# Two small edits in a macaron transformer kernel: the mixing step three units later, and each quarter of x loaded by one request

## The chip, the cores and the metric

The kernel runs on one core of one Trainium2 chip, as one launch. Five engines work side by side and meet at semaphores: TensorE (PE; its weight loads are listed as PEld), VectorE (DVE), ScalarE (ACT), GpSimd (POOL) and SyncE (SP), which here only issues DMA requests. The metric is device time in microseconds, the median of some runs; lower is better. The profile is of one execution, and its times start with the program's span.

## The reference, cut to what matters

Two layers act on x of shape 256 x 1024. Each is a half-weighted SwiGLU feed-forward, a mixer, and a second feed-forward; a norm ends the whole. All weights are f32 in HBM.

```python
for l in range(2):
    x = x + 0.5 * swiglu(rms_norm(x, g1[l]), w_up1[l], w_down1[l])     # 1024 -> 2 x 2816 -> 1024
    x = x + hybrid_mixer(rms_norm(x, g2[l]), ...)                      # proj = h @ w_in, 1024 -> 5888
    x = x + 0.5 * swiglu(rms_norm(x, g3[l]), w_up2[l], w_down2[l])
return rms_norm(x, final_norm)

# in hybrid_mixer: 12 dilated heads in 3 groups of 4, each with its log-sum-exp, and 8 neighbourhood heads
mix_w = softmax(stack(lses), axis=0)                  # weights of the 3 groups, one per head and row
ya = sum(mix_w[..., None] * stack(outs), axis=0)      # dilated branch, 256 columns
yb = neighbourhood_attention(qb, kb, vb, rel_bias)    # 512 columns
merged = sigmoid(gate_a) * (ya @ w_a) + sigmoid(gate_b) * (yb @ w_b)
return merged @ w_out
```

## The kernel before

**Units.** All weights stream through three slots of 128 x 2048 f32 (1 MB a unit). SyncE requests a unit in two DMAs into `raw` (L394), ScalarE rounds it to `w_hi` (L629), VectorE takes the remainder `w_lo = raw - w_hi` (L864), and TensorE multiplies three times (hi x hi, hi x lo, lo x hi: L1207 to L1209 in the mixer, L1270 to L1273 in the feed-forwards). A slot is given back by `split_free` when TensorE has used it. A feed-forward has 33 units, a mixer 30, numbered m = 0 to 29 in each layer.

**The mixer.** Units 0 to 22 are the projection. Attention is put between them: the tables `SCORES_AT`, `TURN_AT`, `TURN_MID`, `VALUES_AT` and `VALUES_MID` say in which unit the scores of a pair of heads, the transposes of their probabilities and the products with v stand, on every engine. Each engine executes its own list in order. Between them VectorE masks scores (L1047), copies the turned probabilities to SBUF (`probs_turned`, L1020; TensorE's products L1442 and its next transposes L1421 wait for that copy), and reads products (`products_read`, L1058 for dilated and L1067 for neighbourhood pairs).

**The mixing.** In unit `MIX_AT`, `mix_weights` (L1082 to L1091, eight small instructions on VectorE, with one Exp on ScalarE, L794, in the middle) makes the group weights `mix_d`. GpSimd waits for them and makes the dilated branch's y in three instructions over all heads (L597, L600, L603). TensorE needs that y in unit `Y_AT` = 22, where it transposes y (L1489). GpSimd has nothing else to do in that time.

**The start.** x lies in SBUF with its rows regrouped by residue modulo 4: partition j of run r holds row 4 j + r, and a run has 64 rows. A quarter of x is 128 partitions (two runs) by 512 columns, 256 KB, and `load_x` (L376) requests it in two DMAs, one a run:

```python
eng.dma_start(runs[i * RUN:(i + 1) * RUN, :], residues(x_in)[r, :, n * NB:(n + 1) * NB])   # 64 x 512 to 64 x 512
```

SyncE requests quarter 0, then the first half of weight block 0 (`first_part(0, 0)`, L463, 512 KB in two requests), quarter 2, `first_part(1, 0)`, quarter 3, `first_part(0, 1)`, `first_part(1, 1)`, then unit 2. Quarter 1 is requested by ScalarE, on its own queue. TensorE transposes the quarters (L1245) in the order 0, 1, 2, with five idle-filling products (`spin`, L1238) after 1 and after 2, and then makes the first products of block 0; quarter 3 is transposed after these, and then the products of block 1's first half. For the second halves it needs `first_part(0, 1)` rounded (`first_hi`, L817) and quarter 3 in `a_both` (L637, L889).

**Requests on GpSimd's queue that a later section looks at.** `na_mask` (L553) and `bias_rows` (L582) are read through a source whose outermost dimension is 4; `v_near` (L592) through one whose outermost dimension is 16:

```python
src = bass.AP(consts.tensor, ..., [[STRIDE * C_ALL, NA_COLS // STRIDE], [0, NA_HEADS], [1, NA_KCOLS]])   # na_mask: 4 x 8 x 32
src = bass.AP(bias_kinds.tensor, ..., [[row * P // STRIDE, STRIDE], [row, P // STRIDE], [1, NA_KEYS]])   # bias_rows: 4 x 32 x 128
near = v_rows[l].rearrange("(g s) n -> g s n", s=RUN // ROWS_N)[:, s0:s0 + NA_KCOLS // STRIDE, :]        # v_near: 16 x 8 x 512
```

Of the kernel before, what the change touches and what calls it, by code (L numbers as in the profile page):

```python
# [12 lines left out]
P = 128  # L13
# [21 lines left out]
RUN = SEQ // STRIDE  # L35
# [7 lines left out]
NB = 512  # L43
# [60 lines left out]
TURN_MID = {12: 3, 14: 5, 17: 7, 19: 9}  # L104
VALUES_AT = {12: (1,), 13: (2, 3), 16: (4, 5), 18: (6, 7), 20: (8, 9)}
VALUES_MID = {10: (0,)}
MIX_AT = 16


def first_of(p):  # L110
# [9 lines left out]
def build(nc, x_in, gains, w_up, w_down, w_in, rel_bias, w_a, w_b, w_out, consts, out):  # L120
# [5 lines left out]
    with ExitStack() as ctx:  # L126
        def sb(name, shape, dt=F32):
            return ctx.enter_context(nc.sbuf_tensor(name, shape, dt))

        def sem(name):  # L130
            return ctx.enter_context(nc.semaphore(name))
# [7 lines left out]
        x = sb("x", [P, TT, D])  # L139
# [77 lines left out]
        x_loaded = [sem(f"x_loaded{g}") for g in range(4)]  # L217
# [91 lines left out]
        def residues(rows):  # L309

            return rows.rearrange("(j r) d -> r j d", r=STRIDE)
# [58 lines left out]
        def load_x(eng, g):  # L370

            t, n = GROUP4[g]
            runs = x[:, t, n * NB:(n + 1) * NB]
            for i in range(P // RUN):
                r = t * (P // RUN) + i
                eng.dma_start(runs[i * RUN:(i + 1) * RUN, :], residues(x_in)[r, :, n * NB:(n + 1) * NB]).then_inc(x_loaded[g], 16)  # L376

        def x_ready(eng, ph, g):

            if ph == 0:  # L380
                eng.wait_ge(x_loaded[g], 16 * P // RUN)
            else:
                eng.wait_ge(x_updated, (ph - 1) * 4 + g + 1)

# [4 lines left out]
        def _(sp):  # L389
# [67 lines left out]
            def first_part(a, h):  # L457

                src = w_up[0].rearrange("l (k p) n -> l p k n", p=P)
                to = raw[a][:, :].rearrange("p (k n) -> p k n", n=FC)  # L460
                for k in (4 * h, 4 * h + 2):
                    arrived = first_arrived if (a, k) == (0, 0) else part_arrived[2 * a + h]
                    sp.dma_start(to[:, k:k + 2, :], src[0, :, k:k + 2, a * D_FF:a * D_FF + FC]).then_inc(arrived, 16)  # L463

            def feed_forward(f, l, at):
# [8 lines left out]
                unit(n0 + F_UNITS - 1, 2, down_unit(f, l, CHUNKS - 1))  # L474

            load_x(sp, 0)
            first_part(0, 0)
            load_x(sp, 2)
            first_part(1, 0)
            load_x(sp, 3)  # L480
            first_part(0, 1)
            first_part(1, 1)
# [31 lines left out]
            for t in range(TT):  # L514
                sp.wait_ge(result_ready, t + 1)
                r = t * P // RUN
# [96 lines left out]
        def _(act):  # L613
            act.dma_start(ident, consts[:, C_IDENT:C_ALL]).then_inc(ident_loaded, 16)
            act.dma_start(gain_rows[0:DEPTH * PHASES * KT, :],
                          gains[0:LAST, :].rearrange("g (k p) -> (g k) p", p=P)).then_inc(gain_rows_loaded, 16)
            load_x(act, 1)

            def hi(l, at, u, c=None):

# [20 lines left out]
            def sum_squares(ph, g):  # L641

                t, n = groups(ph)[g]
                x_ready(act, ph, g)
                if g >= 2:
                    act.wait_ge(squares_done, ph * 4 + g - 1)
                act.activation(squares[:, g % 2 * NB:(g % 2 + 1) * NB], x[:, t, n * NB:(n + 1) * NB], ACT.Square,
                               scale=(1 if ph == LAST else 2) * D ** -0.5,
                               accum_out=half_sums[:, n, t:t + 1]).then_inc(squares_done, 1)
# [77 lines left out]
            def mixer(l):  # L727
                ph = l * PHASES + 1
                input_begin(l, ph, M_AT)
                for m in range(M_UNITS):  # L730
# [42 lines left out]
                    for j, i in enumerate(QK_CHUNKS):  # L773
                        if m == chunk_steps(i)[-1] + 2:
                            act.wait_ge(qkT_done, l * 5 + j + 1)
                            for s in range(2):
# [14 lines left out]
                                act.activation(dst, ft, ACT.Copy, scale=HD ** -0.5 if is_q else 1.0).then_inc(qkT_read, 1)  # L791
                    if m == MIX_AT:
                        act.wait_ge(mix_exp_in, l + 1)
# [49 lines left out]
            for t in range(TT):  # L843
                act.wait_ge(result_ready, t + 1)
                r = t * P // RUN + 1
# [5 lines left out]
        def _(dve):  # L851
# [200 lines left out]
            def products_read(l, p):  # L1052

                at = product_at(2 * p, 0)
                src = bank[OB][:, at:at + 2 * TT * HD].rearrange("p (h t d) -> p h t d", h=2, t=TT)
                if p < DIL_PAIRS:
                    dve.wait_ge(pv_done, l * HEADS + 2 * end_of(p))
                    dve.tensor_copy(o_dil[:, 2 * p:2 * p + 2, :, :], src).then_inc(o_read, 1)  # L1058
                    return
                j = p - DIL_PAIRS  # L1060
                dve.wait_ge(o_read, l * PAIRS + p)
                dve.reciprocal(rden[:, :, :], den[:, 2 * p:2 * p + 2, :]).then_inc(rden_done, 1)
                dve.wait_ge(rden_done, l * (PAIRS - DIL_PAIRS) + j + 1)
                dve.wait_ge(pv_done, l * HEADS + 2 * end_of(p))
                at = GROUP_HEADS * HD + 2 * j * HD
                dst = y[:, :, at:at + 2 * HD].rearrange("p t (h d) -> p h t d", h=2)
                dve.tensor_tensor(dst, src, rden[:, :, :].unsqueeze(3).to_broadcast([P, 2, TT, HD]),  # L1067
                                  ALU.mult).then_inc(o_read, 1)

            def mix_weights(l):  # L1070


                n = [0]
                tops = top[:, 0:DIL_HEADS, :].rearrange("p (g h) t -> p g (h t)", g=GROUPS)
                dens = den[:, 0:DIL_HEADS, :].rearrange("p (g h) t -> p g (h t)", g=GROUPS)

                def chained(ins):
                    ins.then_inc(mix_chain, 1)
                    n[0] += 1
                    dve.wait_ge(mix_chain, l * 6 + n[0])  # L1080
                peak = mix[:, 1, :]
                chained(dve.tensor_tensor(mix[:, 0, :], tops[:, 0, :], tops[:, 1, :], ALU.max))  # L1082
                chained(dve.tensor_tensor(peak, mix[:, 0, :], tops[:, 2, :], ALU.max))
                dve.tensor_tensor(mix_d[:, :, :], tops, peak.unsqueeze(1).to_broadcast([P, GROUPS, GROUP_HEADS * TT]),
                                  ALU.subtract).then_inc(mix_exp_in, 1)
                dve.wait_ge(mix_exp, l + 1)
                chained(dve.tensor_tensor(mix_d[:, :, :], mix_e[:, :, :], dens, ALU.mult))
                chained(dve.tensor_tensor(mix[:, 2, :], mix_d[:, 0, :], mix_d[:, 1, :], ALU.add))
                chained(dve.tensor_tensor(mix[:, 3, :], mix[:, 2, :], mix_d[:, 2, :], ALU.add))
                chained(dve.reciprocal(mix[:, 4, :], mix[:, 3, :]))  # L1090
                dve.tensor_tensor(mix_d[:, :, :], mix_e[:, :, :],  # L1091
                                  mix[:, 4, :].unsqueeze(1).to_broadcast([P, GROUPS, GROUP_HEADS * TT]),
                                  ALU.mult).then_inc(mix_ready, 1)
# [19 lines left out]
            def mixer(l):  # L1113
# [3 lines left out]
                for m in range(M_UNITS):  # L1117
# [20 lines left out]
                    for p in VALUES_MID.get(m, ()):  # L1138
                        products_read(l, p)
                    if m == MIX_AT:  # L1140
                        mix_weights(l)
                    if m == Y_AT:
                        for j in range(3):
                            dve.wait_ge(yT_hi_done, l * 3 + j + 1)
                            for (dst, src), (upper, _) in zip(yT_parts(yT_lo, j), yT_parts(yT_hi, j)):
                                half = dve.tensor_tensor(dst, src, upper.bitcast(F32), ALU.subtract)
                            half.then_inc(yT_lo_done, 1)
# [56 lines left out]
        def _(pe):  # L1204
# [35 lines left out]
            def input_transposes(ph, g):  # L1240
                t, n = GROUP4[g]
                x_ready(pe, ph, g)
                for j in range(4):
                    c = n * NB + j * P
                    tr = pe.transpose(bank[TR[g]][:, j * P:(j + 1) * P], x[:, t, c:c + P], ident)  # L1245
                tr.then_inc(xT_done, 1)
# [397 lines left out]
```

## Time and profile before

| | us |
|---|---|
| median of 3 runs | 1149.88 (1149.08 to 1150.02) |
| the profiled execution | 1150.65 |
| its span | 1148.8 |
| PE busy in the span | 1134.7 (99%) |
| DVE busy | 766.4 (67%) |
| ACT busy | 583.8 (51%) |
| POOL busy | 76.6 (7%) |
| mean granted TensorE clock | 0.998 of full speed |
| DMA, all queues | 214.34 MB, mean 187 GB/s |

A busy time is the sum over an engine's instructions. PE is busy nearly all the time, so what it waits for, and how long, is where a change of order can act; the other engines' idle time costs nothing by itself. `spin` products count as busy, though they do no work of the reference.

### The profile page before, as it was taken

What the parts mean: (1) busy time and instruction counts of PE and PEld (TensorE: products, weight loads), DVE (VectorE), ACT (ScalarE), POOL (GpSimd) and SP (SyncE); (2) the same over time, 40 slices, a digit from 0 to 9 for tenths busy, and PEclk for the clock granted to TensorE, in tenths of its full rate; (3) what the DMA queues carried; (4) which work ended last, traced back from release to release, by engine and by line L of the source; (5) the groups of instructions that cost most, each with busy time, mean ns of one, the idle gap of its engine ahead of it and who ended that gap; (6) DMA issues with size and microseconds to landing.
All of it is one profiled execution on the core that took longest, in us unless ns stands there. A gap on an engine that the chain in (4) does not pass through costs nothing.

```text
span 1148.8 us, 17172 instructions
## 1 busy us (share of the span) xinstructions
PE 1134.7 (99%) x6707; PEld 955.3 (83%) x6707; DVE 766.4 (67%) x981; ACT 583.8 (51%) x781; POOL 76.6 (7%) x116
## 2 busy tenths in 40 slices
PE   8999999999999999999999999999999999999997
PEld 6888888888878888888888888888887888888886
DVE  5866667756666676666686666677566577666665
ACT  6444445555544654444474444465555545544442
POOL 3622100000110000000000000000003000000000
PEclk9999999999999999999999999999999999999999
DMA  9866654744544565556556555656446546655551
GB/s 288 276 208 229 205 191 147 256 150 145 191 161 145 183 220 183 184 190 207 171 165 216 183 183 185 201 189 199 152 143 198 202 131 201 202 196 184 184 182 37
DMA packets 148246, 214.34 MB, mean 187 GB/s; under 512 B 9344, under 2 KB 114016, under 8 KB 147936
## 3 DMA queue, kind: packets, MB, share of 16 engines
q1 hardware_dynamic: 142960, 205.28, 53.9%
q0 software_dynamic: 4560, 6.97, 2.1%
q10 hardware_dynamic: 672, 1.37, 0.4%
q8 instruction: 34, 0.56, 0.2%
q14 instruction: 20, 0.16, 0.0%
HBM read 210.75 MB, written 5.12 MB: 188 GB/s over the span
## 4 chain that ended last, share of the span: by engine, by line
PE 94%; DVE 2%; issue 1%; ACT 1%; DMA 1%; SPq 0%; POOLq 0%; POOL 0%; DVEq 0%; ACTq 0%
PE banks L1273 25%; PE banks L1207 16%; PE banks L1209 15%; PE banks L1208 15%; PE banks L1271 14%; PE banks L1270 3%; PE banks L1421 1%; PE banks L1384 1%; PE banks L1245 1%; PE banks L1407 1%; PE banks L1453 1%; DMA raw<-ffn_w_up_dram 1%; DVE w_lo L864 1%; ACT w_hi L629 1%; DVE probs L1047 0%
## 5 line engine op out<-in xcount | busy, mean ns | idle before, releaser
L864 DVE TENSOR_TENSOR w_lo<-raw,w_hi 128x2048 fp32r<-128x2048 f32 x190 | 438.8, 2310 | 192.7 <-ACT w_hi L629 192.4
L629 ACT ACTIVATE w_hi<-raw 128x2048 fp32r<-128x2048 f32 x190 | 363.6, 1915 | 212.2 <-PE banks L1209 210.1
L1273 PE MATMUL banks<-a_both,w_hi 128*128 128x512 f32 x1232 | 439.4, 396 | 0.0
L1271 PE MATMUL banks<-a_both,w_lo 128*128 128x256 f32 x1408 | 364.3, 279 | 0.7 <-DVE a_both L889 0.7
L1271 PEld LDWEIGHTS banks<-a_both,w_lo 128*128 128x128 f32 x1408 | 265.4, 189 | 15.7 <-issue 1.0
L1273 PEld LDWEIGHTS banks<-a_both,w_hi 128*128 128x128 f32 x1232 | 231.2, 188 | 47.3
L1207 PE MATMUL banks<-w_hi,a_both 128*128 128x512 f32 (+1 forms) x448 | 176.6, 394 | 0.0
L1209 PE MATMUL banks<-w_hi,a_both 128*128 128x512 f32 (+1 forms) x448 | 171.6, 383 | 0.0
L1208 PE MATMUL banks<-w_lo,a_both 128*128 128x512 f32 (+1 forms) x448 | 171.2, 382 | 0.0
L1207 PE MATMUL banks<-w_hi,hT_hi 128*128 128x512 f32 x320 | 125.0, 390 | 0.0
L1209 PE MATMUL banks<-w_hi,hT_lo 128*128 128x512 f32 x320 | 124.5, 389 | 0.0
L1208 PE MATMUL banks<-w_lo,hT_hi 128*128 128x512 f32 x320 | 124.5, 389 | 0.0
L1209 PEld LDWEIGHTS banks<-w_hi,a_both 128*128 128x128 f32 x448 | 84.2, 188 | 17.0
L1207 PEld LDWEIGHTS banks<-w_hi,a_both 128*128 128x128 f32 x448 | 84.3, 188 | 16.3 <-issue 1.3
L1208 PEld LDWEIGHTS banks<-w_lo,a_both 128*128 128x128 f32 x448 | 84.4, 189 | 14.6
L687 ACT ACTIVATE gates<-banks 128x512 f32<-128x512 f32 x44 | 26.3, 598 | 118.1 <-PE banks L1273 118.1
L694 ACT ACTIVATE gates<-banks 128x512 f32<-128x512 f32 x44 | 26.4, 600 | 101.7 <-PE banks L1273 101.7
L1209 PEld LDWEIGHTS banks<-w_hi,hT_lo 128*128 128x128 f32 x320 | 60.1, 188 | 12.7
L1208 PEld LDWEIGHTS banks<-w_lo,hT_hi 128*128 128x128 f32 x320 | 60.1, 188 | 12.6
L1270 PE MATMUL banks<-a_both,w_hi 128*128 128x512 f32 x176 | 70.1, 398 | 0.0
L1207 PEld LDWEIGHTS banks<-w_hi,hT_hi 128*128 128x128 f32 x320 | 60.1, 188 | 10.8
L937 DVE TENSOR_TENSOR gates<-banks,gates 128x512 f32<-128x512 f32 x44 | 30.4, 691 | 47.5 <-ACT gates L687 47.5
(119 smaller groups left out, 927.4 us busy)
## 6 DMA issues: line engine op xcount, KB each, us to landing
raw<-ffn_w_up_dram SPq DMA_DIRECT2D x172, 512.0 KB, 4.2
raw<-w_in_dram SPq DMA_DIRECT2D x92, 512.0 KB, 4.5
raw<-ffn_w_down_dram SPq DMA_DIRECT2D x88, 512.0 KB, 4.0
raw<-w_out_dram SPq DMA_DIRECT2D x16, 512.0 KB, 4.3
raw<-w_branch_b_dram SPq DMA_DIRECT2D x8, 512.0 KB, 4.4
raw<-ffn_w_up_dram SPq DMA_DIRECT2D x8, 256.0 KB, 5.9
bias_rows<-bias_kinds POOLq DMA_DIRECT2D x32, 64.0 KB, 4.0
bias<-bias_rows SPq DMA_DIRECT2D x2, 1024.0 KB, 7.2
```

The costliest lines, as they stand in the source:

```text
L629: act.activation(w_hi[slot][:, :], raw[slot][:, :], ACT.Copy).then_inc(hi_done, 1)
L687: act.activation(u_low, U_BANKS[:, :, SEQ:2 * SEQ], ACT.Copy).then_inc(u_low_done, 1)
L694: act.activation(v_low, V_BANKS[:, :, SEQ:2 * SEQ], ACT.Copy).then_inc(v_low_done, 1)
L864: dve.tensor_tensor(w_lo[slot][:, :], raw[slot][:, :], w_hi[slot][:, :].bitcast(F32), ALU.subtract).then_inc(lo_done, 1)
L937: dve.tensor_tensor(u_sum, U_BANKS[:, :, 0:SEQ], u_low, ALU.add).then_inc(u_read, 1)
L1207: pe.matmul(dst, s_hi, m_hi, start=start, stop=False)
L1208: pe.matmul(dst, s_hi, m_lo, start=False, stop=False)
L1209: return pe.matmul(dst, s_lo, m_hi, start=False, stop=stop)
L1245: tr = pe.transpose(bank[TR[g]][:, j * P:(j + 1) * P], x[:, t, c:c + P], ident)
L1270: mm = pe.matmul(pair[:, b, :], w, both, start=True, stop=False)
L1271: mm = pe.matmul(pair[:, b, 0:SEQ], w_lo[slot][:, at:at + P], a_hi[:, k, :], start=False, stop=False)
L1273: mm = pe.matmul(pair[:, b, :], w, both, start=False, stop=k == KT - 1)
```

## The change

It has two independent parts. `MIX_AT` goes from 16 to 19, so that the group weights are made at the end of unit 19, and GpSimd's three instructions follow them. And `load_x` makes one request for a quarter in place of two; quarter 1 is requested by SyncE right behind quarter 0, and no longer by ScalarE.

```diff
-MIX_AT = 16
+MIX_AT = 19
@@ load_x
             t, n = GROUP4[g]
-            runs = x[:, t, n * NB:(n + 1) * NB]
-            for i in range(P // RUN):
-                r = t * (P // RUN) + i
-                eng.dma_start(runs[i * RUN:(i + 1) * RUN, :], residues(x_in)[r, :, n * NB:(n + 1) * NB]).then_inc(x_loaded[g], 16)
+            r = t * (P // RUN)
+            rows = residues(x_in)[r:r + P // RUN, :, n * NB:(n + 1) * NB]
+            eng.dma_start(x[:, t, n * NB:(n + 1) * NB], rows).then_inc(x_loaded[g], 16)
@@ x_ready
-                eng.wait_ge(x_loaded[g], 16 * P // RUN)
+                eng.wait_ge(x_loaded[g], 16)
@@ SyncE
             load_x(sp, 0)
+            load_x(sp, 1)
             first_part(0, 0)
@@ ScalarE
-            load_x(act, 1)
```

The source of a request before is 64 rows of 512; the source of one after is 2 x 64 x 512 (run, row, column), and its destination 128 partitions of 512.

On VectorE, around units 16 and 17 of the first mixer, before: `mix`, `mix_d` are the group weights, `probsT` the turned probabilities.

```order
L1058 COPY o_dil<-banks 128x256 x2
L864 TENSOR_TENSOR w_lo<-raw,w_hi 128x2048
L1082 TENSOR_TENSOR mix<-top 128x8
L1083 TENSOR_TENSOR mix<-mix,top 128x8
L1084 TENSOR_TENSOR mix_d<-top,mix 128x24
L1087 TENSOR_TENSOR mix_d<-mix_e,den 128x24
L1088 TENSOR_TENSOR mix<-mix_d 128x8
L1089 TENSOR_TENSOR mix<-mix,mix_d 128x8
L1090 RECIPROCAL mix<-mix 128x8
L1091 TENSOR_TENSOR mix_d<-mix_e,mix 128x24
L1020 COPY probsT<-banks 128x512
L864 TENSOR_TENSOR w_lo<-raw,w_hi 128x2048
```

After, the same place (line numbers are one less):

```order
L1057 COPY o_dil<-banks 128x256 x2
L863 TENSOR_TENSOR w_lo<-raw,w_hi 128x2048
L1019 COPY probsT<-banks 128x512
L863 TENSOR_TENSOR w_lo<-raw,w_hi 128x2048
L1019 COPY probsT<-banks 128x512
```

And after, at the end of unit 19, where the eight instructions now stand:

```order
L1019 COPY probsT<-banks 128x512
L1081 TENSOR_TENSOR mix<-top 128x8
L1082 TENSOR_TENSOR mix<-mix,top 128x8
L1083 TENSOR_TENSOR mix_d<-top,mix 128x24
L1086 TENSOR_TENSOR mix_d<-mix_e,den 128x24
L1087 TENSOR_TENSOR mix<-mix_d 128x8
L1088 TENSOR_TENSOR mix<-mix,mix_d 128x8
L1089 RECIPROCAL mix<-mix 128x8
L1090 TENSOR_TENSOR mix_d<-mix_e,mix 128x24
L1061 RECIPROCAL rden<-den 128x4
L1066 TENSOR_TENSOR y<-banks,rden 128x2x2x64
```

They moved from ahead of the copies and the split of unit 17 to a place behind the last copy of unit 19 and ahead of unit 20's reading of products.

SyncE's first requests, before:

```order
L376 DMA x<-x_dram 64x512 x2
L463 DMA raw<-ffn_w_up_dram 128x2x256 x2
L376 DMA x<-x_dram 64x512 x2
L463 DMA raw<-ffn_w_up_dram 128x2x256 x2
L376 DMA x<-x_dram 64x512 x2
L463 DMA raw<-ffn_w_up_dram 128x2x256 x4
```

And after:

```order
L375 DMA x<-x_dram 128x1x512 x2
L462 DMA raw<-ffn_w_up_dram 128x2x256 x2
L375 DMA x<-x_dram 128x1x512
L462 DMA raw<-ffn_w_up_dram 128x2x256 x2
L375 DMA x<-x_dram 128x1x512
L462 DMA raw<-ffn_w_up_dram 128x2x256 x4
```

The first row is now quarters 0 and 1, one request each (the shape shown is the destination's).

## Rows read from the trace of the kernel before

**Rows 1.** The page: busy us, share of the span, instructions.

```profile
PE 1134.7 (99%) x6707; PEld 955.3 (83%) x6707; DVE 766.4 (67%) x981; ACT 583.8 (51%) x781; POOL 76.6 (7%) x116
```

**Rows 2.** Waits of PE by cause: us in total, times, longest.

```profile
PE banks L1245 <- DMA x<-x_dram: 2.0, 2, 1.6
PE banks L1442 <- DVE probsT L1020: 1.8, 2, 0.9
...
PE banks L1421 <- DVE probsT L1020: 0.5, 2, 0.3
```

**Rows 3.** Timeline of PE, first mixer: start, us, engine, line, operation.

```profile
314.10 0.39 PE L1208 MATMUL banks<-w_lo,a_both 128*128 128x512 f32 x1
314.32 0.39 PE L1209 MATMUL banks<-w_hi,a_both 128*128 128x512 f32 x1
314.98 0.63 PE L1421 MATMUL banks<-cst,probs 128*128 128x128 f32 x4 [0.27 <-DVE probsT L1020]
...
318.30 0.65 PE L1442 MATMUL banks<-v_near,probsT 128*32 128x64 f32 x32
319.87 0.65 PE L1442 MATMUL banks<-v_near,probsT 128*32 128x64 f32 x32 [0.92 <-DVE probsT L1020]
...
333.58 1.10 PE L1442 MATMUL banks<-v_near,probsT 128*32 128x64 f32 x64
...
344.27 0.92 PE L1489 MATMUL banks<-cst,y 128*128 128x128 f32 x7
```

**Rows 4.** Timeline of DVE, first mixer, units 16 to 20.

```profile
310.11 2.28 DVE L864 TENSOR_TENSOR w_lo<-raw,w_hi 128x2048 fp32r<-128x2048 f32 x1
...
314.04 0.18 DVE L1091 TENSOR_TENSOR mix_d<-mix_e,mix 128x24 f32<-128x24 f32 x1
...
314.98 4.23 DVE L864 TENSOR_TENSOR w_lo<-raw,w_hi 128x2048 fp32r<-128x2048 f32 x1
319.14 0.68 DVE L1020 COPY probsT<-banks 128x512 f32<-128x512 f32 x1
...
334.82 0.42 DVE L1067 TENSOR_TENSOR y<-banks,rden 128x256 f32<-128x256 f32 x1 [2.79 <-PE banks L1442]
```

**Rows 5.** Timeline of POOL in the same stretch.

```profile
314.30 2.76 POOL L597 TENSOR_TENSOR o_dil<-o_dil,mix_d 128x1536 f32<-128x1536 f32 x1 [7.53 <-DVE mix_d L1091]
317.14 3.20 POOL L600 TENSOR_TENSOR o_dil<-o_dil 128x512 f32<-128x512 f32 x1
320.42 1.27 POOL L603 TENSOR_TENSOR y<-o_dil 128x512 f32<-128x512 f32 x1
```

**Rows 6.** Stretches of the start: PE, PEld, DVE, ACT, POOL busy, clock, DMA share, GB/s.

```profile
8.00:10.00 2.00, 1.63 (x10) 0.88 (x9) 0.97 (x5) 2.00 (x6) 0.00 (x0) 1.00 1.11 300
12.00:14.00 2.00, 2.00 (x13) 1.71 (x13) 1.23 (x1) 2.00 (x8) 0.00 (x0) 1.00 1.09 383
```

**Rows 7.** DMA queues, 305 to 312 us: packets, MB, share of 16 engines.

```profile
q0 software_dynamic: 320, 1.05, 50.1%
```

**Rows 8.** The same view, 55.5 to 58 us.

```profile
q0 software_dynamic: 316, 0.26, 40.6%
```

**Rows 9.** The same view, 33.4 to 34.2 us, with its packet sizes.

```profile
DMA packets 98, 0.21 MB, mean 262 GB/s; under 512 B 44, under 2 KB 48, under 8 KB 98
...
q0 software_dynamic: 32, 0.00, 7.8%
```

**Rows 10.** x's first request, issued at 0.76: us to landing.

```profile
DMA to landing us min/median/max: 2.9/2.9/2.9
```

**Rows 11.** Timelines of PE and ACT at the start.

```profile
9.41 0.66 PE L1245 MATMUL banks<-cst,x 128*128 128x128 f32 x4 [0.37 <-DMA x<-x_dram]
11.04 0.47 PE L1270 MATMUL banks<-a_both,w_hi 128*128 128x512 f32 x1
...
14.53 1.06 ACT L817 ACTIVATE w_hi<-raw 128x1024 fp32r<-128x1024 f32 x1
...
18.04 0.36 PE L1271 MATMUL banks<-a_both,w_lo 128*128 128x256 f32 x1 [0.70 <-DVE a_both L889]
```

## Prediction

> **What bounds the kernel now.** I read the page's busy line first: PE is busy 1134.7 of 1148.8 us [rows 1], so only what delays PE can move the time, by at most the 14.1 us that are left and whatever a new wait adds. Second, the waits of PE by cause [rows 2]. At the start PE waits for x (2.0 us in two pieces), and in each of the two mixers it waits for VectorE's copies of turned probabilities (L1442, L1421). No row has PE waiting for weights. Once started PE streams, so a delay at the start goes through to the end unshortened, and so does a wait removed from a mixer.
>
> **Part one: the mixing leaves unit 16.** In the timeline of PE [rows 3] the two transposes' neighbours show the price. L1421 starts at 314.98, 0.66 after the product ahead of it, where that one started 0.22 after its own predecessor: 0.43 lost, to the nearest step. The first half of L1442 starts at 318.30 and the second at 319.87, 1.57 later; all 64 of such products take 1.10 at 333.58, so half take 0.55: 1.02 lost. Together 1.45 a mixer, and rows 2 count these waits twice, so 2.9 us.
>
> Why VectorE was late [rows 4]: the eight small instructions hold it from the end of a split at 312.3 to 314.22 (1.9 us), ahead of the copy that L1421 wants. Then the split at 314.98 takes 4.23 where the one at 310.11 takes 2.28. What is beside it: GpSimd's L597 starts at 314.30 the moment the weights are there, runs 2.76, and its L600, a third of the size, takes 3.20, against 1.27 of the equally large L603 that stands beside an idle VectorE [rows 5]. VectorE and GpSimd hold each other up. So the copy that L1442 wants starts only at 319.14. Without mixing in unit 16 the copy runs at 312.3 to 313.0, the split follows and ends by 315.4, and the last copy is done at 316.1, where PE wants it at about 318.4: both waits go, with 2 us to spare. The split's input w_hi comes earlier too, since ScalarE's Exp of the mixing stood ahead of its rounding.
>
> What is late next: nothing in units 17 and 18, since PE's following items have no wait row at all. At the new place, the end of unit 19, VectorE waits 2.79 us for PE (ahead of L1067) [rows 4], and the 1.9 us fit into that; behind it in its queue stand unit 20's reading of products and the split of unit 22, which PE wants a unit and a half later. GpSimd is the one with a date. Everything there is 1.45 earlier: VectorE is free at 334.82 - 2.79 - 1.45 = 330.6, the weights are ready at 332.5, GpSimd needs 7.4 as before (314.30 to 321.69, with both engines' collisions in it), so y is there at 339.9; PE wants it at 344.27 - 1.45 = 342.8 [rows 3]. The margin is 2.9 us. I cost the new place at nothing; if that cover went, it costs what exceeds 2.9, in each mixer. Bounds of part one: -2.9 and, with both collisions moved onto something that PE wants, 0. I take -2.9, since the rows ahead of and behind both places are PE's own.
>
> **Part two: the requests for x.** What it saves on the issuing side is small: three request slots of SyncE and two of ScalarE, about 0.6 us each, in a stretch where the 16 DMA engines are full (share 1.11 and 1.09 in [rows 6]). With the same spreading over the engines I would give it between 0 and -1 us, as the quarters' requests come earlier but their bytes don't move faster.
>
> The point is the spreading. The source of a request was 64 rows; now its outermost dimension is 2 (two runs of 64 rows). The trace has no such request on SyncE's queue, but it has on GpSimd's. Four requests of `v_near`, 16 x 8 rows, 256 KB each, make 320 packets for 1.05 MB [rows 7]. Four of `bias_rows`, 4 x 32 rows, 64 KB each, make 316 (and some on the window's edge) for 0.26 MB [rows 8]: as many packets for a quarter of the bytes. And one of `na_mask`, outermost 4, 4 KB, makes 32 packets [rows 9], while of all packets in that window just 48 - 44 = 4 are between 512 B and 2 KB: the 4 KB are in four pieces, and the rest carry nothing. So the number of engines that carry data is that of the outermost dimension where it is under 16. That is GpSimd's queue, and that SyncE's does the same is my choice; by it each quarter of x goes through 2 of 16 engines.
>
> The Trainium skill says it for both: in "DMA: Bandwidth & Descriptors", "Why a DMA increments its semaphore by 16 and not by 1", the number of engines is the largest up to 16 that divides the slowest dimension over 1 of both access patterns; of 2 and 128 that is 2, on the lowest-numbered engines. The trace agrees for 4 (rows 8, 9), and no run here yet shows it for 2. If its rule held on GpSimd's queue alone, the sum would be the rival's of 1146.5 below.
>
> Price, as work of the two engines, which serve their requests in order. In 12 to 14 us the 16 move 383 GB/s, 23.9 each [rows 6]. A quarter is 131 072 B an engine: 5.48 us. A pair of weight requests spread over 16 gives each 32 768 B: 1.37. The first request of x took 2.9 [rows 10], of which 8192 B at this rate are 0.34, so 2.56 are fixed. Landings: quarter 0 at 0.76 + 2.56 + 5.48 = 8.8; quarter 1 14.3; block 0's first half 15.7; quarter 2 21.1; block 1's 22.5; quarter 3 28.0; `first_part(0, 1)` 29.4; `first_part(1, 1)` 30.7; unit 2 (1 MB, 2.74) 33.5. The rest of each request, on 14 engines, is there long before.
>
> What PE makes of it [rows 11]: its first products come 1.63 behind quarter 2, at 22.8 (before 11.04), and are done before quarter 3 is there. Then the chain that ended last before: ScalarE rounds `first_part(0, 1)`, scales quarter 3, VectorE makes the remainder, PE goes on at 18.04, 3.51 after the 14.53 at which the rounding began. Now 29.4 + 3.5 = 32.9. The delay is 14.8. Unit 2 at 33.5 comes 0.6 behind that point, and PE wants it only after two more half blocks, so it adds nothing, and from there on all requests wait for PE's progress as before. Bounds of the rate an engine reaches: 18.8 GB/s from 8 to 10 us, a stretch with x in it (300/16), gives a quarter 6.99 and a pair 1.74, and a delay of 22.0; from above, a share of 1.09 to 1.11 says that packets overlap within an engine, and one that has no neighbours might gain as much once more, 26.5, which gives a quarter 4.95, a pair 1.24 and a delay of 12.3. I take 23.9, measured where the queues are never short of work and hold no x.
>
> **Sum.** -2.9 + 14.8 = +11.9 against the profiled execution's span, 1148.8 to 1160.7, its time 1150.65 to 1162.5. That execution is 0.8 over the median of the runs, so the median goes from 1149.9 to **1161.8**.
>
> **The rivals.**
> *Sixteen engines all the same* (faster). SyncE's queue would spread 128 rows by the destination, or by rows flattened. For it: all requests of SyncE in the trace keep the engines full, and none shows fillers. Against: [rows 8, 9]. Then PE gets -2.9 and up to -1 at the start: 1146.0 to 1147.0, say 1146.5.
> *TensorE at its lower level.* The granted clock is 1.00 in every stretch of the start, with PE's waits for x up to 1.6 us [rows 2, 6]. Now it idles about 5 us between quarters. Its work from 11.04 to 18.04 is 7.0 less the wait of 0.70 [rows 11], two parts of some 3 us. At 1.2 instead of 2.4 GHz each takes 6: the first ends at 28.8, hidden up to 0.8 behind quarter 3; the second at 35, 2.1 after 32.9; if the next is slow too, 3 more. 1163.9 to 1166.9, say 1165. The Trainium skill's "TensorE: Matmul & The Clock Gate", Part 1, has such a fall for an idle array; that it lasts is not to be read from here.
> *Slow engines*: each of the two at 18.8 GB/s, as in the crowded stretch; +22.0 - 2.9: 1169.
> *y comes late*: GpSimd is held up beyond 10.3 us at its new place by VectorE's splits and reads, and PE waits at unit 22 what it no longer waits at 17 and 18. It decides from the margin of 2.9. With part two's price: up to 1164.7.
>
> **Chances.** Forecast 0.63, its own range 1158 to 1166; lower level 0.11; slow engines 0.06; y late 0.03; sixteen engines 0.15; smaller mixtures 0.02. The range 1155 to 1170 holds all cases but the sixteen engines and tails. A measurement of this kernel can tell 0.2% (2.3 us) from no change: faster 0.14, same 0.02 (a smaller price that cancels part one), slower 0.84.
>
> **What would show it.** Right: the requests of x take 8 us and more to land, PE's first L1270 at 21 to 24 us instead of 11.04, PE's stretch of waits ends at about 33 instead of 18.04; fewer packets of 4 B on SyncE's queue in the first microseconds; waits of L1442 and L1421 for `probsT` gone from the list; the split behind the first copy of unit 17 takes 2.3; GpSimd starts L597 at about 332.5 + 14.8 and the L1489 that follows waits for nothing. Wrong: x landing within 5 us (then the rival of 1146.5), a granted clock under 1.00 in the first 35 us with products 0.46 apart, a new wait of L1489 for `y`, or a PE that waits for `w_lo` behind unit 2.

## The result and the profile after

| | before | after |
|---|---|---|
| median, us | 1149.82 (1149.08 to 1150.02, 4 runs) | 1161.45 (1161.36 to 1162.62, 4 runs) |
| profiled execution: its span | 1148.8 | 1159.6 |
| mean granted TensorE clock | 0.998 | 0.992 |

The ratio is 1.0102 with a 95% interval of 1.0088 to 1.0116: slower by 11.6 us, where 1161.8 was predicted. The rows below are of the profile after; its line numbers are mostly one less than before.

Busy time by engine on the page, against [rows 1]:

```profile
PE 1137.1 (98%) x6707; PEld 956.9 (83%) x6707; DVE 764.7 (66%) x981; ACT 583.4 (50%) x781; POOL 77.8 (7%) x116
```

PE has as many instructions, and the span grew by 10.8 while PE's busy time grew by 2.4: it waits. The waits of PE by cause, against [rows 2]:

```profile
PE banks L1244 <- DMA x<-x_dram: 11.4, 4, 3.9
PE banks L1237 <- DVE warm L852: 1.2, 1, 1.2
PE banks L1270 <- DVE a_both L888: 1.2, 1, 1.2
PE banks L1588 <- DMA gain_rows<-gains_dram: 0.9, 1, 0.9
```

The wait for x went from 2.0 us in two pieces to 11.4 in four, one per quarter. Both rows for `probsT` are gone, and none for `y` has come. PE's timeline at the start, against [rows 11]:

```profile
9.51 1.12 PE L1244 MATMUL banks<-cst,x 128*128 128x128 f32 x4 [3.85 <-DMA x<-x_dram]
14.41 1.11 PE L1244 MATMUL banks<-cst,x 128*128 128x128 f32 x4 [3.79 <-DMA x<-x_dram]
...
20.88 0.92 PE L1244 MATMUL banks<-cst,x 128*128 128x128 f32 x4 [3.22 <-DMA x<-x_dram]
...
23.37 0.99 PE L1269 MATMUL banks<-a_both,w_hi 128*128 128x512 f32 x1
...
27.60 0.66 PE L1244 MATMUL banks<-cst,x 128*128 128x128 f32 x4 [0.53 <-DMA x<-x_dram]
...
32.27 0.36 PE L1270 MATMUL banks<-a_both,w_lo 128*128 128x256 f32 x1 [1.20 <-DVE a_both L888]
```

Quarter after quarter is there 4.9 us or more behind the last. The last row is the end of the waits, at 18.04 before: 14.23 later. What released it is the same chain as before (ScalarE rounds `first_part(0, 1)` and scales quarter 3, VectorE makes the remainders). In ScalarE's timeline:

```profile
28.77 1.06 ACT L816 ACTIVATE w_hi<-raw 128x1024 fp32r<-128x1024 f32 x1 [3.34 <-DMA raw<-ffn_w_up_dram]
```

`first_part(0, 1)` is there at 28.77, and PE goes on 3.50 later (3.51 before). One thing differs: here ScalarE waited for the landing, and before its rounding at 14.53 waited for nothing. The stretches of the start show why, against [rows 6] (the same columns):

```profile
8.00:10.00 2.00, 0.49 (x3) 0.50 (x4) 0.00 (x0) 0.00 (x0) 0.00 (x0) 0.50 0.46 160
10.00:12.00 2.00, 0.62 (x3) 0.22 (x2) 0.02 (x1) 1.14 (x4) 0.00 (x0) 0.50 0.13 51
...
16.00:18.00 2.00, 1.66 (x4) 0.29 (x2) 1.26 (x5) 1.74 (x5) 0.00 (x0) 0.57 0.13 51
18.00:20.00 2.00, 0.00 (x0) 0.00 (x0) 1.06 (x2) 0.00 (x0) 0.00 (x0) 1.00 0.51 146
```

A DMA share of 0.13 is two of 16 engines, moving 51 GB/s together, where the share was 1.1 before. (0.13 is what two engines give if each is busy all the time; that it is two is counted in e5 to e7.) The DMA queues from 10 to 12 us, the view of [rows 7 to 9]:

```profile
DMA packets 50, 0.10 MB, mean 51 GB/s; under 512 B 0, under 2 KB 0, under 8 KB 50
```

Only rows of x of 2 KB move: 25 an engine in 2 us, 25.6 GB/s each. The same rows show what the prediction had as a rival: the granted clock is 0.50, TensorE's lower level of 1.2 GHz, in much of the time between quarters (it reads 1.00 from 18 to 20 us, behind 1.66 us of work).

SyncE's timeline has something nobody asked for:

```profile
0.75 1.30 SPq L375 DMA_DIRECT2D x<-x_dram  x2
2.09 5.07 SPq L462 DMA_DIRECT2D raw<-ffn_w_up_dram  x2
7.20 1.26 SPq L375 DMA_DIRECT2D x<-x_dram  x1
8.51 4.97 SPq L462 DMA_DIRECT2D raw<-ffn_w_up_dram  x2
13.52 1.16 SPq L375 DMA_DIRECT2D x<-x_dram  x1
```

Two weight requests took 1.10 us to issue before (2.02 to 3.12), and take 5.07 now: SyncE stands at a request, it seems while the two engines work off what is queued. Quarter 2 is asked for only at 7.20 and quarter 3 at 13.52. That raised the question of whether the engines or SyncE's stalls cost the time (run e11).

In the first mixer, VectorE's timeline, against [rows 4]:

```profile
326.20 0.68 DVE L1019 COPY probsT<-banks 128x512 f32<-128x512 f32 x1
326.80 2.28 DVE L863 TENSOR_TENSOR w_lo<-raw,w_hi 128x2048 fp32r<-128x2048 f32 x1
...
348.15 2.96 DVE L863 TENSOR_TENSOR w_lo<-raw,w_hi 128x2048 fp32r<-128x2048 f32 x1
```

The split between the copies takes 2.28 and no longer 4.23. GpSimd's three, against [rows 5], and PE's y, against the last of [rows 3]:

```profile
346.20 2.76 POOL L597 TENSOR_TENSOR o_dil<-o_dil,mix_d 128x1536 f32<-128x1536 f32 x1 [25.50 <-DVE mix_d L1090]
349.04 3.23 POOL L600 TENSOR_TENSOR o_dil<-o_dil 128x512 f32<-128x512 f32 x1
352.35 1.30 POOL L603 TENSOR_TENSOR y<-o_dil 128x512 f32<-128x512 f32 x1
```

```profile
356.59 1.47 PE L1488 MATMUL banks<-cst,y 128*128 128x128 f32 x12
```

y is there at 353.65 and wanted at 356.59 without a wait: a margin of 2.94. The collision moved with the mixing, to a split (348.15, 2.96) that nobody waits for.

### The profile page after: what moved, and what is told of

Same layout as the page of the kernel before. It is cut to its first block, busy times and chain, and to the rows that moved or that the text cites. A ratio compares the mean times of both kernels' runs of the same rounds, so it can differ in the third digit from the quotient of the medians.

```text
span 1159.6 us, 17168 instructions
## 1 busy us (share of the span) xinstructions
PE 1137.1 (98%) x6707; PEld 956.9 (83%) x6707; DVE 764.7 (66%) x981; ACT 583.4 (50%) x781; POOL 77.8 (7%) x116
## 2 busy tenths in 40 slices
DMA packets 148126, 214.34 MB, mean 185 GB/s; under 512 B 9224, under 2 KB 113896, under 8 KB 147816
## 4 chain that ended last, share of the span: by engine, by line
PE 96%; SPq 1%; DMA 1%; DVE 0%; issue 0%; ACT 0%; POOLq 0%; POOL 0%; DVEq 0%
PE banks L1272 25%; PE banks L1206 16%; PE banks L1208 16%; PE banks L1207 16%; PE banks L1270 14%; PE banks L1269 3%; SPq L462 1%; PE banks L1420 1%; DMA raw<-ffn_w_up_dram 1%; PE banks L1383 1%; PE banks L1244 1%; PE banks L1406 1%; PE banks L1452 1%; PE banks L1395 0%; PE banks L1441 0%
## 5 line engine op out<-in xcount | busy, mean ns | idle before, releaser
L1206 PEld LDWEIGHTS banks<-w_hi,hT_hi 128*128 128x128 f32 x320 | 60.1, 188 | 10.8
```

Source lines behind the costliest of these rows:

```text
L1206: pe.matmul(dst, s_hi, m_hi, start=start, stop=False)
```

## The experiments

Each median stands beside that of the kernel before from runs on the same chip. PE's restart is the start of the product with which PE went on at 18.04 before, in the profiled execution of each kernel.

| run | median, us | before | ratio (95%) | PE's restart |
|---|---|---|---|---|
| e1_mix19 | 1147.18 | 1150.14 | 0.9974 (0.9965 to 0.9984) | 17.75 |
| e2_xonly | 1165.38 | 1150.14 | 1.0132 (1.0117 to 1.0146) | 33.07 |
| e3_pool_late | 1149.16 | 1150.14 | 0.9993 (0.9984 to 1.0002) | 17.78 |
| e4_mix20 | 1155.35 | 1150.14 | 1.0052 (1.0040 to 1.0064) | 18.10 |
| e5_outer4 | 1154.46 | 1150.16 | 1.0038 (1.0024 to 1.0052) | 23.82 |
| e6_outer8 | 1148.88 | 1150.16 | 0.9991 (0.9981 to 1.0000) | 20.43 |
| e7_outer16 | 1146.34 | 1150.16 | 0.9970 (0.9960 to 0.9981) | 17.31 |
| e8_split2_sp | 1146.95 | 1150.16 | 0.9974 (0.9965 to 0.9984) | 17.52 |
| e9_warm_after | 1161.67 | 1150.23 | 1.0100 (1.0085 to 1.0116) | 33.80 |
| e10_outer8_warm | 1148.90 | 1150.23 | 0.9992 (0.9983 to 1.0001) | 20.60 |
| e11_x_on_act | 1167.53 | 1150.23 | 1.0149 (1.0134 to 1.0165) | 38.56 |
| e12_one_merged | 1152.80 | 1150.23 | 1.0023 (1.0013 to 1.0032) | 23.88 |

### e1_mix19: the mixing alone

```diff
-MIX_AT = 16
+MIX_AT = 19
```

(on the kernel before)

> The kernel before with MIX_AT = 19 alone, the loads of x untouched. Theory (the two parts are independent and TensorE streams between them): both mixers lose the waits of L1442 and L1421 for probsT, so -2.9 to -3.2 us against before, about 1146.7, and the split behind unit 17's first copy takes 2.3 us. Rival (the gain seen after is a side effect of the later start, which gave the weight stream a lead): under 1 us, and waits for probsT remain.

Measured: 2.96 us faster. The waits of PE in full, but for one on the `spin` weights:

```profile
PE banks L1245 <- DMA x<-x_dram: 2.1, 2, 1.3
...
PE banks L1271 <- DVE a_both L889: 0.7, 1, 0.7
```

Nothing of the mixer is left in the list. By start times of the same products, the two transposes win 0.45 and the two products 1.15 in each mixer. Part one is a gain by itself.

### e2_xonly: the requests alone

```diff
-MIX_AT = 19
+MIX_AT = 16
```

(on the kernel after)

> The changed kernel with MIX_AT back at 16, so that only the requests for x differ from before. Theory: +14.2 us against before (TensorE's restart at 32.3 instead of 18.0), about 1164.0, with the two waits for probsT in each mixer as before. Rival (part of the later start is absorbed by slack in the first feed-forward): under +12.

Measured: 15.24 us slower than before; PE restarts 15.03 later. Its list of waits has the mixer's back:

```profile
PE banks L1244 <- DMA x<-x_dram: 11.4, 4, 4.0
PE banks L1441 <- DVE probsT L1019: 1.8, 2, 0.9
...
PE banks L1420 <- DVE probsT L1019: 0.5, 2, 0.3
```

The parts add within 0.7: 15.24 - 2.96 = 12.3 against 11.6 for both. The text had 14.2.

### e3_pool_late: GpSimd out of the way, VectorE's mixing left in place

```diff
-                pool.wait_ge(o_read, l * PAIRS + DIL_PAIRS)
+                pool.wait_ge(o_read, l * PAIRS + PAIRS - 1)
```

(on the kernel before: GpSimd starts on y only when VectorE has read the products of all pairs but one; the eight small instructions stay in unit 16)

> The kernel before (mixing in unit 16, old loads), but GpSimd's three mixing instructions also wait until the ninth pair of products has been read (unit 20). Separates the two parts of VectorE's lateness. Theory (the collision with GpSimd makes L1442 wait, the eight small instructions make L1421 wait): the split at unit 17 takes 2.3 instead of 4.2, the wait of L1442 goes (1.0 a mixer), the wait of L1421 stays (0.3 to 0.4 a mixer): -2.0 us against before. Rival (the eight instructions and ScalarE's Exp alone make the delay): no gain, -0.3 to 0.

Measured: 0.98 us less in the median, with an interval that just includes no change, and 1.5 less in the span of the profiled execution. The text had 2.0. What it shows is in the trace. VectorE's timeline:

```profile
314.68 2.29 DVE L864 TENSOR_TENSOR w_lo<-raw,w_hi 128x2048 fp32r<-128x2048 f32 x1 [0.15 <-ACT w_hi L629]
...
334.38 4.47 DVE L864 TENSOR_TENSOR w_lo<-raw,w_hi 128x2048 fp32r<-128x2048 f32 x1
```

and the waits of PE in the mixers:

```profile
PE banks L1489 <- POOL y L603: 0.8, 2, 0.4
PE banks L1421 <- DVE probsT L1020: 0.5, 2, 0.3
```

Without GpSimd beside it the split of unit 17 takes 2.29 (4.23 in [rows 4]), and the wait of L1442 is gone: by start times 1.10 is won there in each mixer. The one of L1421 stays, since the eight small instructions still stand ahead of its copy. So the price of the old place was two: about 1.1 a mixer by the collision, 0.43 by the queue. The collision now meets the split at 334.38, y comes 0.4 late, and the gain is half lost. The Trainium skill, "SBUF — State Buffer", "Who interferes with whom", says that a VectorE instruction with two inputs in SBUF contends with a GpSimd instruction that reads SBUF; the trace agrees, 2.29 against 4.47 for the same split.

### e4_mix20: the mixing one unit too late

```diff
-MIX_AT = 16
+MIX_AT = 20
```

(on the kernel before)

> The kernel before with MIX_AT = 20: the mixing one unit past the new place, behind the split of unit 22. Tests the margin of y. Theory: the weights are ready some 7 us later than at 19, GpSimd needs 5.4 to 7.4, so y comes 1.5 to 4 us after TensorE wants it at unit 22: a new wait ahead of L1489 of that length in each mixer, and in all 0 to +5 us against before. Rival (GpSimd is fast enough away from VectorE's work): same as e1, -3 us.

Measured: 5.2 us slower in the median. PE's timeline in the first mixer, of an execution of 1158.74:

```profile
346.31 2.82 PE L1489 MATMUL banks<-cst,y 128*128 128x128 f32 x12 [3.04 <-POOL y L603]
348.78 0.78 PE L1207 MATMUL banks<-w_hi,a_both 128*128 128x512 f32 x1
```

and its stretches (clock third from the end):

```profile
343.00:346.00 3.00, 0.27 (x2) 0.00 (x0) 1.48 (x2) 1.91 (x1) 2.92 (x2) 0.90 0.41 132
346.00:349.00 3.00, 2.69 (x13) 2.69 (x14) 3.00 (x2) 1.26 (x3) 0.25 (x1) 0.50 0.54 217
349.00:352.00 3.00, 3.00 (x9) 2.32 (x9) 1.51 (x5) 0.66 (x2) 0.00 (x0) 0.50 0.86 288
352.00:355.00 3.00, 3.00 (x14) 2.50 (x13) 0.00 (x0) 0.00 (x0) 0.00 (x0) 0.96 0.15 61
```

y is 3.0 late in each mixer, which confirms the place's date: one unit more uses up the margin of 2.94 and as much again. But a wait of 3.04 costs more than 3.04. Behind it the granted clock is 0.50 for some six us; in the second mixer, behind an equal wait, for some three. Against e1's profiled 1147.26 this one has 6.1 of waits and 5.4 more. The six runs went from 1155.06 to 1159.63, four of them near 1155.2, so that price seems to vary between executions; why was not tried.

### e5, e6, e7: outermost dimension 4, 8, 16

```diff
-            r = t * (P // RUN)
-            rows = residues(x_in)[r:r + P // RUN, :, n * NB:(n + 1) * NB]
+            rows = x_in[t * P:(t + 1) * P, n * NB:(n + 1) * NB].rearrange("(j r) d -> r j d", r=4)
```

(on the kernel after; r=8 and r=16 in the other two. These three, and e10, load the rows of each half of x in another order, so their values are not the reference's; they serve for their times.)

> The changed kernel, each quarter of x still one request of 128 rows of 2 KB, but read through a source whose outermost dimension is 4 (4 x 32 rows, others of the same half of x, so the values differ from the reference's). Theory (a request's data goes over as many engines as the outermost dimension, each at some 24 GB/s): a quarter is 2.7 us of an engine, quarter 0 lands at about 6.1, first_part(0, 1) at 18.4, TensorE's restart at 21.9 (+3.9), with the mixers' -3.2 in all about +0.7: 1150.5 us. Rival (the cost is of one big request, or of SyncE's queue, whatever the shape): as the changed kernel, 1161.5.

> As before, outermost dimension 8 (8 x 16 rows; values differ from the reference's). Theory: a quarter is 1.4 us of an engine, first_part(0, 1) lands at about 12.9, hardly another time than in the kernel before; restart at 17.5 to 18.5, total -2.5 to -3.5 against before, 1146.5 to 1147.5. Rival: 1161.5.

> As before, outermost dimension 16 (16 x 8 rows; values differ from the reference's): one request a quarter over all engines, which the change wanted. Theory: quarters land at 4.0 to 9, restart at 17 to 18, total -3.0 to -4.2 against before: 1146 to 1147. Rival: 1161.5.

Measured: 1154.46, 1148.88 and 1146.34 us. The pages count the packets; here after (2), then the three:

```profile
DMA packets 148126, 214.34 MB, mean 185 GB/s; under 512 B 9224, under 2 KB 113896, under 8 KB 147816
```

```profile
DMA packets 148134, 214.34 MB, mean 186 GB/s; under 512 B 9232, under 2 KB 113904, under 8 KB 147824
```

```profile
DMA packets 148150, 214.34 MB, mean 187 GB/s; under 512 B 9248, under 2 KB 113920, under 8 KB 147840
```

```profile
DMA packets 148182, 214.34 MB, mean 187 GB/s; under 512 B 9280, under 2 KB 113952, under 8 KB 147872
```

The bytes are the same, and of packets under 512 B there are 9216 + 4 x 2, + 4 x 4, + 4 x 8, + 4 x 16; before has 9344 = 9216 + 8 x 16 (and e12, one request of 2 and six of 64 rows, has 9314 = 9216 + 2 + 6 x 16; only e2's page, 9225, has one more than its 9224). So each request of x ends with one small packet for each engine that it uses, and the engines are as many as its outermost dimension. The Trainium skill, "DMA: Bandwidth & Descriptors", "Why a DMA increments its semaphore by 16 and not by 1", says the same of requests by SyncE: the engines used post the increments, and the sequencer the rest. The times follow the bytes an engine carries. Compared with 16, x puts 65,536 B more on each engine that it uses at 8, three times that at 4 and seven times at 2; the medians are 2.5, 8.1 and 15.1 above 1146.34, so 2.2 to 2.7 us for each 65,536 B, where 65,536 B at the 23.9 GB/s of [rows 6] are 2.74. Both e5 and e6 restarted later than their texts have it, by 1.9 at least; e10 and e12 ask why.

### e8_split2_sp: two requests a quarter, all by SyncE

```diff
             load_x(sp, 0)
+            load_x(sp, 1)
             first_part(0, 0)
...
-            load_x(act, 1)
```

(on e1_mix19; a request is 64 rows again)

> MIX_AT = 19 and quarter 1 requested by SyncE right behind quarter 0, but every quarter in two requests of 64 rows as before. It is the other half of the change to the loads, and a version with the reference's values. Theory (the place in the queues hardly matters where all 16 engines are full): quarter 1 lands up to 1 us earlier, the weights behind it up to 1 us later, restart within 0.5 of 18.0: the same as MIX_AT = 19 alone (1147.2), within 0.7. Rival (two queues side by side are served faster than one): 1 us or more slower than that.

Measured: 1146.95, the same ratio as e1's, and PE restarts at 17.52. That quarter 1 is asked for by SyncE costs and gains nothing that these runs can tell; all that the second part costs lies in the shape of its requests. One request a quarter over all engines (e7) is even 0.6 us faster than this: eight of its nine runs, on the same chip, lie under the fastest of these ten.

### e9_warm_after: TensorE kept busy between the quarters

```diff
-                        spin(5)
+                        spin(22 if g == 1 else 5)
...
-            spin(8)
+            spin(28)
...
+            spin(18)
```

(on the kernel after: more idle-filling products ahead of quarter 0 and behind quarters 0 and 1)

> The changed kernel with more idle-filling products: 28 instead of 8 at the very start, 18 behind the first quarter's transposes, 22 instead of 5 behind the second's. They fill TensorE's waits for x, in which its granted clock went to 0.50. Theory (the lower level is hidden behind the wait for quarter 3 and first_part(0, 1), which set TensorE's restart at 32.3): clock 1.00 up to 24 us, first product at 22.5 instead of 23.4, restart and total unchanged within 0.4 us of 1161.5. Rival (the lower level costs part of the delay): 1 us or more faster.

Measured: 1161.67, against 1161.45. Its stretches of the start, where after had 0.50 to 0.57 in six of the eight from 8 to 24 us:

```profile
8.00:14.00 6.00, 5.37 (x27) 2.58 (x26) 1.33 (x5) 1.14 (x4) 0.00 (x0) 1.00 0.37 127
14.00:20.00 6.00, 5.26 (x27) 2.49 (x26) 2.33 (x6) 2.18 (x6) 0.00 (x0) 1.00 0.38 127
20.00:26.00 6.00, 4.89 (x28) 3.27 (x27) 1.23 (x1) 2.33 (x6) 0.00 (x0) 1.00 0.63 186
```

The upper level is kept up to 28 us and nothing is won in the median, so the lower level in the kernel after lies under the wait for x: 0.53 of that wait is left there ahead of quarter 3. The profiled execution itself is the slowest of the four, 1163.00 against 1161.49 to 1161.80. In it the x quarters came later (the first product at 23.69, not the text's 22.5; quarter 3 at 28.93), the clock fell behind quarter 3, and PE's restart was 33.80 without a wait. The rounding behind the wait began at 29.95, and 3.50 on makes 33.45, so some 0.35 of the lower level is not hidden in this execution.

### e10_outer8_warm: the same for outermost 8

```diff
-                        spin(5)
+                        spin(12 if g == 1 else 5)
...
-            spin(8)
+            spin(10)
...
+            spin(5)
```

(on e6_outer8)

> The run with outermost dimension 8 (values differ from the reference's in the same way) with more idle-filling products: 10 instead of 8, 5 behind the first quarter, 12 instead of 5 behind the second. There the granted clock was 0.50 from 8 to 15 us and TensorE's restart came at 20.4 where 17.5 to 18.5 was expected. Theory (that miss is the clock's): clock 1.00 throughout, restart at 18.0 to 18.5, total 2 us under the 1148.9 of that run. Rival (eight engines simply deliver late): restart stays at 20.4, same total.

Measured: 1148.90, the same as e6's 1148.88, with a granted clock of 1.00 in every stretch from 7 to 16 us, where e6 had 0.50 to 0.77 from 8 us on. By the medians, then, my reason for e6's miss falls. What stays is the first half of block 1. ScalarE's timelines, first before, then e6 and e10:

```profile
11.34 1.06 ACT L817 ACTIVATE w_hi<-raw 128x1024 fp32r<-128x1024 f32 x1 [1.16 <-DMA raw<-ffn_w_up_dram]
```

```profile
12.59 1.06 ACT L815 ACTIVATE w_hi<-raw 128x1024 fp32r<-128x1024 f32 x1 [2.40 <-DMA raw<-ffn_w_up_dram]
```

```profile
13.90 1.06 ACT L815 ACTIVATE w_hi<-raw 128x1024 fp32r<-128x1024 f32 x1 [3.18 <-DMA raw<-ffn_w_up_dram]
```

In e8 the same rounding starts at 10.82. In before, e1, e7, e8 and e10 PE's restart is 6.70 or 6.71 behind it (18.04 - 11.34), so a late first half of block 1 arrives there whole. Each weight request also has its share on the eight engines that carry x, and is done only when these are: the three quarters queued ahead of this one put 49,152 B more on each, 2.06 us at 23.9 GB/s, and it came 1.77 and 3.08 behind e8's. The two profiled executions don't agree further. In e6 the restart is 7.84 behind the rounding, and PE waits for nothing:

```profile
20.43 0.28 PE L1269 MATMUL banks<-a_both,w_lo 128*128 128x256 f32 x1
```

There the slow products of the lower level ended last and cost 1.14; in e10 that is gone, but the half block itself was 1.31 later. Why it was, and what share each has in the medians, is not shown.

### e11_x_on_act: the quarters on ScalarE's queue

```diff
-            load_x(sp, 0)
-            load_x(sp, 1)
             first_part(0, 0)
-            load_x(sp, 2)
...
-            load_x(sp, 3)
...
+            for g in range(4):
+                load_x(act, g)
```

(on the kernel after: SyncE requests weights alone)

> The changed kernel (outermost 2, one request a quarter) with all four quarters requested by ScalarE, so that SyncE's weight requests do not stand behind them. SyncE's requests for weights took up to 3.7 us each to issue in the changed kernel. Theory (the two engines' total work sets the delay, whichever queue asks): weights land earlier but x later, as the engines take turns: quarter 2 at 21 to 28, quarter 3 at 28 to 33, restart at 32 to 38, total 1161 to 1167. Rival (SyncE's blocked issuing is the cost): restart before 28, total under 1157.

Measured: 1167.53, 17.3 over before and 6.1 over after, half a microsecond past the text's range; PE's restart, 38.56, is past it too. The timeline of SyncE:

```profile
0.76 4.44 SPq L462 DMA_DIRECT2D raw<-ffn_w_up_dram  x8
```

and of ScalarE:

```profile
1.72 13.54 ACTq L375 DMA_DIRECT2D x<-x_dram  x4
15.30 1.28 ACT L818 ACT_TABLE_LOAD   x1 [15.30 <-issue]
```

SyncE is free to issue eight requests in 4.44 us, and the kernel is slower still: PE gets quarters 0 to 2 at 15.27, 22.91 and 29.32, and turns quarter 3 at 35.31 without a wait. So SyncE's stalls are not what costs. The two engines are: from 16 to 24 us the DMA share is 0.13 or 0.14 with 49 to 51 GB/s, and ahead of that the weights requested early must have had their share on them. The stall did not vanish, it went with x: ScalarE took 13.54 to issue four requests, and its first instruction waited behind them.

### e12_one_merged: one quarter merged, three not

```diff
+            if g == 0:
+                rows = residues(x_in)[r:r + P // RUN, :, n * NB:(n + 1) * NB]
+                eng.dma_start(x[:, t, n * NB:(n + 1) * NB], rows).then_inc(x_loaded[g], 16)
+                return
             for i in range(P // RUN):
...
```

(on e8_split2_sp; only quarter 0 is one request with outermost 2)

> The changed kernel with only quarter 0 in one request of outermost 2, the other three in two requests of 64 rows each, all on SyncE's queue. Theory (each such quarter adds its own time on two engines, 4.9 us by the landings of the changed kernel, less 0.7 to 1 of its time over 16): restart 3.5 to 4.5 later than the 17.5 of the version with eight requests of 64 rows, total 1150.5 to 1151.5. Rival (the first such request already blocks the queue for all): most of the 14 us, over 1157.

Measured: 1152.80, 5.85 over e8. PE's timeline:

```profile
11.21 2.38 PE L1249 MATMUL banks<-cst,x 128*128 128x128 f32 x8 [4.56 <-DMA x<-x_dram]
```

One merged request makes its own quarter late, until 11.21, and PE turns it and the one behind it in one go. The end shifts by 5.85: more than the 4.80 us that 114,688 B more on each of two engines make at 23.9 GB/s, and more than the text's 1151.5. The trace has the rest. PE waits for nothing from 11.21 to its restart, and it is slow there:

```profile
13.38 2.34 PE L1242 MATMUL banks<-warm 128*128 128x512 bf16 x5
```

Five such products take 1.24 at the upper level and 2.34 in the kernel after at a granted clock of 0.50. (The stretch rows of e12 read 1.00 here; the products' own times are the surer sign.) ScalarE rounds block 1's first half at 15.70 and the restart is 23.88, 8.18 behind, where 6.70 is the rule without slow products. So an estimate of 1.48 is TensorE's, and 22.40 - 17.52 = 4.88 is left for the two engines. Against e8 the four cost 14.5, not four times 5.85. That PE has work to do while the later quarters load would explain it; no run takes this apart.

## Why the prediction was right, and where it was not

**The bound.** PE streams from its restart on, and a delay at the start arrives whole: 14.23 at the restart, -1.59 and -1.57 in the mixers, -0.28 in small pieces, 10.8 in the span. Right.

**Part one** was forecast at -2.9; the profile has -3.2 (the 1.59 and 1.57) and e1 alone -2.96. Both its causes are shown apart by e3. The margin of y was forecast at 2.9 and is 2.94; e4 shows the price beyond it. Costing the new place at nothing was right, though both collisions went along.

**Two of 16 engines.** That SyncE's queue spreads as GpSimd's does in [rows 7 to 9] was the chosen assumption, with 0.15 for the rival of sixteen engines. The share of 0.13, the eight small packets (two for each of four requests), and the series 2, 4, 8, 16 show it. What one request a quarter saves with all engines was given as between 0 and -1; e7 against e8 has -0.6.

**The landings.** Two terms were mis-sized and partly cancel. The engine's rate was taken as 23.9 GB/s; quarters 0 and 1 came 4.90 apart (5.48 was forecast), which is 26.7, past the upper bound of 26.5. Other executions with the same requests have 5.15 (e2) and 5.28 (e9), 25.5 and 24.8 GB/s, between the choice and the bound. The fixed part of the first request was 2.56 from [rows 10]; 9.51 - 0.75 - 4.90 leaves 3.86, and e2 and e9 leave 4.4 and 4.5. Forecast and measured: quarter 0 8.8 and 9.51, quarter 1 14.3 and 14.41, quarter 2 21.1 and 20.88, quarter 3 28.0 and 27.60, `first_part(0, 1)` 29.4 and 28.77. The restart came at 32.27 where 32.9 stood. By the restarts of e2 and e1 the requests cost 15.3 (14.8 forecast, on a restart at 18.04; e1, e3 and e4, with the old requests, have 17.75, 17.78 and 18.10). That the total came within 0.4 us of the forecast is partly luck: the faster engine, the longer fixed part and the spread between executions, about 1 us in the landings, cancel.

**TensorE at its lower level** was a rival and half true: the clock did fall to 0.50, the first product at 23.37 was slow, the work behind quarter 3 was not, and by e9's median it costs nothing here. What the rival missed is where the idle time ends: ahead of quarter 3 PE waited only 0.53. Its chance should have been on "falls, and is hidden". It is not hidden in every execution: in e9's profiled one the second part was slow, as the rival had it, and PE was 1.5 later at its restart, of which 1.2 is the later landing. The prediction also took the rows' 1.00 at the start at its word. PE's first eight `spin` products took 3.60 in before, 0.45 each, against 0.25 in the five from 7.80 on, so TensorE began at its lower level.

**Not foreseen at all:** SyncE's stalled requests. They changed nothing, since each quarter's request was still made ahead of the engines' reaching it (quarter 3's at 13.52, for data that moved from about 27.60 - 4.90 = 22.7 on). That was luck of the order and not part of the working.

**Slow engines** at 18.8 GB/s did not occur. With neighbours an engine was slower all the same: at outermost 4 quarters 0 and 1 came 3.0 apart for 65,536 B, 21.8 GB/s, and e5, whose `first_part(0, 1)` came at 20.31 and not at 18.4, was late by the engines alone. e6 and e12 came out later than forecast too, in part by TensorE's slow products. How an engine's rate depends on the others stays open.

## What to carry to other kernels

Merging two requests into one can narrow the transfer: look at the outermost dimension of the new access pattern, since a request with 2 there used 2 of 16 engines here and put everything queued behind it, weights too, at their pace. Count the small packets on the page to see how many engines a request used. And a small instruction can be expensive through what it lets start: here VectorE's eight took 1.9 us, but two thirds of their price was GpSimd beginning beside a split; with both parts apart, the first alone is the better kernel (e1 and e8, 0.26% under before), and the second is worth 0.6 us where it is done with full width (e7). Read TensorE's level off the times of equal products, beside the clock's rows.

## What the runs showed of the hardware that I had not expected

- A request can hold its issuer: after requests of x over two engines, one weight request's issue took 3.67 us in the kernel after, and four requests of x by ScalarE 13.54 us (0.5 to 0.65 each before). The pair of weight requests behind quarter 2 took 4.97 us at outermost 2, 3.42 at 4, 1.15 at 8 and 1.10 at 16.
- One wait of 3.04 us in a stream that had run at a granted clock of 1.00 was followed by 0.50 for some six us (e4), while keeping TensorE busy through the idle stretches at the start of after and e6 won nothing in the median (e9, e10).
- In e9 the clock, kept at 1.00 by more products up to 28 us, was 0.61 in 30 to 34, behind a wait of 2.10 for quarter 3. That execution took 1163.00 us, 1.3 over the median.
